# A hybrid decoder step as one list of stages, with compression rows by position and decode parts in column groups

## What is computed

```python
z = rmsnorm(x, pre_norm) @ w_in                 # 3652 columns in layer 0, 6924 in layer 1
# layer 0: differential attention (A, 4 heads, two maps each, softmax1 - lam * softmax2)
#          and indexer-sparse attention (B): the 256 (decode) or 64 (prompt) best keys of
#          score = sum_h w_h * relu(q_idx_h . k_idx), then softmax over those
# layer 1: NSA (C): compressed blocks, selected blocks and a window of 512, mixed by gates,
#          and dilated attention (D): three groups (128, 1), (512, 4), (2048, 16)
def compress(rows, pos_emb, w1, w2):            # C: blocks of 32 rows, 16 apart
    blocks = rows[:, idx] + pos_emb             # (n, 32, 128)
    hid = gelu(einsum('bnrd,rdh->bnh', blocks, w1))
    return hid @ w2
mix = concatenate([o_left * silu(g_left), o_right * silu(g_right)])
y = x + rmsnorm(mix @ w_out, post_norm)
```

## Time and profile before

| | |
|---|---|
| median of 3 runs | 1359.72 us (1356.55 to 1361.18) |
| span of the profiled execution | 1352.9 us; no time of its own beside the span is given for it |
| instructions | 10043 |
| PE busy | 1068.6 us (79%) |
| DVE busy | 417.7 us (31%) |
| ACT busy | 257.1 us (19%) |
| POOL busy | 100.1 us (7%) |
| moved by the transfers | 213.99 MB, a mean of 158 GB/s |

### The profile page before, as it was taken

One profiled execution on the slowest core, in us unless ns is written; L12 is line 12 of the kernel. 1 busy time (PEld: TensorE's weight loads), 2 busy tenths in 40 slices (PEclk: granted clock), 3 DMA queues, 4 the chain that ended last, 5 costly groups with the idle time before them and its releaser, 6 DMA issues.

```text
span 1352.9 us, 10043 instructions
## 1 busy us (share of the span) xinstructions
PE 1068.6 (79%) x3730; PEld 445.2 (33%) x3730; DVE 417.7 (31%) x834; ACT 257.1 (19%) x521; POOL 100.1 (7%) x140
## 2 busy tenths in 40 slices
PE   0799975995995398996675779949999978878586
PEld 0433331221233133332123333323333444455332
DVE  1007655003567021872221310021212144232513
ACT  2511210110025000110030321111010112434112
POOL 2000002001101000001310000010000120100000
PEclk9999986995895589897687879979897965969779
DMA  6424656004999701004836357375444352213330
GB/s 256 162 98 158 241 203 220 0 12 137 360 330 345 275 1 62 1 0 192 367 125 233 131 184 281 123 254 184 171 159 178 101 174 85 86 63 125 94 124 32
DMA packets 71152, 213.99 MB, mean 158 GB/s; under 512 B 6128, under 2 KB 26352, under 8 KB 67648
## 3 DMA queue, kind: packets, MB, share of 16 engines
q0 software_dynamic: 12160, 119.47, 24.0%
q1 hardware_dynamic: 58944, 93.88, 20.4%
HBM read 207.31 MB, written 64.68 MB: 201 GB/s over the span
## 4 chain that ended last, share of the span: by engine, by line
PE 69%; issue 9%; ACT 8%; DVE 6%; DMA 4%; another core or an unknown queue 2%; SPq 1%; ACTq 0%; DVEq 0%
PE psum L580 27%; PE psum L541 14%; PE psum L510 6%; PE psum L764 4%; PE psum L590 3%; PE psum L850 3%; PE psum L672 2%; DMA ring<-in_cmp_w 2%; PE psum L648 2%; PE psum L598 2%; ACT Z L1358 2%; PE psum L521 1%; DMA ring<-in_w_out_even 1%; ACT PT L1232 1%
## 5 line engine op out<-in xcount | busy, mean ns | idle before, releaser
L580 PE MATMUL psum<-ring,XB 128*128 128x512 f32 (+2 forms) x832 | 370.6, 602 | 13.3 <-DMA ring<-in_w_out_even 11.1
L541 PE MATMUL psum<-Z,ring 128*128 128x512 f32 x256 | 225.6, 1038 | 10.9 <-DMA ring<-in_cmp_w 10.9
L580 PEld LDWEIGHTS psum<-ring,XB 128*128 128x128 f32 x832 | 159.2, 199 | 225.1 <-issue 205.4
L1158 ACT COPY Z<-psum 128x512 f32<-128x512 f32 (+3 forms) x78 | 43.6, 559 | 385.1 <-PE psum L580 359.0
L541 PEld LDWEIGHTS psum<-Z,ring 128*128 128x128 f32 x256 | 54.1, 221 | 137.4 <-issue 125.0
L510 PE MATMUL psum<-const,ring 128*128 128x128 f32 (+1 forms) x352 | 71.7, 342 | 9.0 <-issue 4.5
L1501 DVE TENSOR_TENSOR RT<-Z,const 128x256 f32<-128x256 f32 (+10 forms) x25 | 8.7, 347 | 199.2 <-ACT Z L1158 198.5
L510 PEld LDWEIGHTS psum<-const,ring 128*128 128x128 f32 (+1 forms) x352 | 46.8, 165 | 67.2 <-issue 53.2
L1628 DVE CUSTOM_DVE_ANT_0 SM<-psum,const 128x128 f32<-128x128 f32 (+4 forms) x48 | 18.9, 394 | 123.2 <-PE psum L648 118.0
L672 PE MATMUL psum<-Z,PT 128*128 128x128 f32 x168 | 31.6, 335 | 24.5 <-ACT PT L1232 23.6
L590 PE MATMUL psum<-ring,XB 128*32 128x512 f32 (+2 forms) x416 | 50.6, 588 | 0.0
(11 more groups left out here) (286 smaller groups left out, 934.5 us busy)
## 6 DMA issues: line engine op xcount, KB each, us to landing
ring<-in_w_in_odd SPq DMA_DIRECT2D x13, 2048.0 KB, 12.3
ring<-in_cmp_w SPq DMA_DIRECT2D x8, 2048.0 KB, 10.5
ring<-in_w_in_even SPq DMA_DIRECT2D x7, 2048.0 KB, 7.8
out_s_d_k<-in_state_d_k POOLq DMA_DIRECT2D x8, 1022.0 KB, 11.5
out_s_d_v<-in_state_d_v POOLq DMA_DIRECT2D x8, 1022.0 KB, 10.6
ring<-in_w_out_even SPq DMA_DIRECT2D x2, 2048.0 KB, 12.6
ring<-in_state_d_k SPq DMA_DIRECT2D x2, 2048.0 KB, 8.8
ring<-in_state_d_v SPq DMA_DIRECT2D x2, 2048.0 KB, 12.0
```

Of the source, the lines that this page charges most:

```text
L541: last = mm(out[:, h * 512:(h + 1) * 512], w[:, (r % 16) * CH + h * 128:(r % 16) * CH + h * 128 + 128], ap(rowsT[:, r:r + 1], [CS, 512]), ...
L580: last = mm(out[:, 0:n], xT[:, k, t * 128:(t + 1) * 128], w[:, k * n:(k + 1) * n], start=k == 0, stop=k == KT - 1)
L1158: copy(dst, pp[0:dst.shape[0], 0:n]).then_inc(P.free, 1)
```

## The change

- Both layers are one list of stages, `ORDER`, made by `even_order` and `odd_order`. Each engine's program has a function for each kind of stage and goes through that one list. A unit's work is four stages (`prep`, `scores`, `probs`, `output`) that stand in different places of the list.
- Weights have two buffers of 2 MB. Gathered rows and other transfers of about 1 MB have buffers of their own: two fixed ones, and others that are lent for a stretch of the list by tensors that lie idle in it (`homes`).
- `rowsT` becomes 16 planes of 520 columns, one for each position modulo the stride. `compress` reads 512 neighbouring columns; the position vectors stand in column 511 of each plane, and the bias is read from column 511 of the result.
- `decode_rows` gives each of the four groups of output partitions a quarter of the chunk's columns and runs the whole contraction; there is no folding matmul. ACT copies four quarters.
- The keys of shared decode parts go in four column groups, one batch row in each, for 256 keys at a time; softmax then runs on 128 rows.
- Queries reach all partitions by transposes of a repeated column, and for A by a copy to SBUF.
- Chunks are taken in another order, and gates are applied from PSUM before ACT frees the bank (`copy_z`, which is ACT's). The prompt's "sel" units come before "cmp".
- At the start, X, the identity and the rest of the constants are loaded apart, and the page table in one transfer.

```diff
-        items, place, released = [], {}, {}
-
-        def item(name, queue, parts):
-            place[name] = (len(items) % SLOTS, None)
-            items.append((name, queue, parts))
+        def weights(name, parts, at=None):
+            if at is None:
+                at = len([n for n, queue, _ in items if queue == "sp"]) % 2
+            before = [last_weights[at]] if last_weights[at] else []
+            last_weights[at] = name
+            item(name, "sp", parts, f"weights{at}", ring[:, at * 2 * PART:(at + 1) * 2 * PART], before)
...
+        homes = [dict(slot="rows0", view=ring[:, 4 * PART:5 * PART], span=(0, len(ORDER)), before=[], only=None),
+                 dict(slot="rows1", view=ring[:, 5 * PART:6 * PART], span=(0, len(ORDER)), before=[], only=None),
+                 dict(slot="probs", view=PD[:, :], span=(step_of["turn_x", 0, 2], step_of["a_scores", 0]),
+                      before=["turn_x0"], only=None),
+                 dict(slot="heads", view=flat[:, 1024:3072], span=(step_of["scores", 11], step_of["soft", "b"]),
+                      before=["heads_read"], only=None),
...
             def compress(kv):
...
-                        last = mm(out[:, h * 512:(h + 1) * 512],
-                                  w[:, (r % 16) * CH + h * 128:(r % 16) * CH + h * 128 + 128],
-                                  ap(rowsT[:, r:r + 1], [CS, 512]), start=r == 0, stop=r == CB - 1)
+                out, w = turned["out", kv], slot_of(name)
+                at = (r % 16) * PLANE + r // 16
+                for h in range(2):
+                    last = mm(out[:, h * 512:(h + 1) * 512],
+                              w[:, (r % 16) * CH + h * 128:(r % 16) * CH + h * 128 + 128],
+                              rowsT[:, at:at + 512], start=r == BLK_ORDER[0], stop=r == BLK_ORDER[-1])
...
-            def decode_rows(w, n):
-
-                pe.wait_ge(P.free, P.claim())
-                out = P.filling
-                for k in range(KT):
-                    g = 32 * (k % 4)
-                    last = mm(out[g:g + 32, 0:n], xTs[:, k, :], w[:, k * n:(k + 1) * n], start=k < 4, stop=k >= 4)
-                last.then_inc(P.full, 1)
+            def decode_rows_of(w, n):
+
+                pe.wait_ge(T.free, turned["x", 2])
+                pe.wait_ge(P.free, P.claim())
+                out, q = P.filling, n // 4
+                for k in range(KT):
+                    for g in range(4):
+                        last = mm(out[32 * g:32 * g + 8, 0:q], xTs[:, k, :], w[:, k * n + g * q:k * n + (g + 1) * q],
+                                  start=k == 0, stop=k == KT - 1)
+                last.then_inc(P.full, 1)
...
-            def broadcast_query(zs, q, b):
...
-                mm(out[:, :], ap(C("one8", 8)[:, b:b + 1], [0, 128]), zs[0:8, q:q + 512],
-                   start=True, stop=True).then_inc(O.full, 1)
+            def on_all_rows(bank, b):
+
+                pe.wait_ge(T.free, turned["queries"])
+                pe.wait_ge(bank.free, bank.claim())
+                for h in range(H):
+                    last = tr(bank.filling[:, h * 128:(h + 1) * 128], ap(QB[:, h, b:b + 1], [0, 128]))
+                last.then_inc(bank.full, 1)
...
-                        last = mm(out[0:32, half * 512:(half + 1) * 512], QD[0:w, b, :],
-                                  KTs[l][0:w, (i - 1) % 2, :], start=b == 0 and not masked, stop=b == NB - 1)
+                    for q in range(4):
+                        last = mm(DB.filling[32 * q:32 * q + 32, pair * 256:pair * 256 + 256], QD[0:w, 4 * j + q, :],
+                                  KTs[0:w, q, :], start=j + pair == 0 and kind != "c", stop=j + pair == 2)
...
+            def own(kind):
...
+                for b in range(NB):
+                    g = 32 * (b % 4)
+                    last = mm(O.filling[g:g + 32, 0:8], QD[0:w, b, :], KN[0:w, :], start=b < 4, stop=b >= 4)
...
+            def copy_z(l, i, t):
...
+                if w:
+                    act(z[:, c + at:c + at + w], pp[0:n, at:at + w], ACT.Tanh, scale=0.5).then_inc(sem("gate_tanh"), 1)
+                    eng.wait_ge(sem("gate_tanh"), count(sem("gate_tanh")))
+                    eng.wait_ge(sem("gated"), due("act", "gated"))
+                    eng.sem_inc(P.free, 1)
...
+        MOVED_AFTER = dict(ak=1, ck=2, cv=2, dk=2, wk=2, wv=2, ak0_0=0, ak0_1=0, rows1_2=4, bv_3=4)
+        MOVED_AFTER.update({f"ak{b}_{half}": 2 for b in (5, 6, 7) for half in (0, 1)})
...
+                if name == "wout0_1":
+                    sp.wait_ge(*marks["keys_used", "b", TILES["b"] - 1])
+                    load_norm(NW[:, :], "post_norm", 0, "post_in")
+                    sp.wait_ge(*marks["mixed", 0])
+                    load_norm(NWP, "pre_norm", 1, "pre_in")
...
+            for event in ORDER:
+                if event[0] in stages:
+                    stages[event[0]](*event[1:])
```

3169 lines of the change are left out of this document (1662 added, 1507 removed).

## The result

The kernel after takes 935.35 us (median of 4 runs, 930.02 to 937.64), the kernel before 1360.04 us in the same comparison. The ratio is 0.6877, its 95% interval 0.6853 to 0.690.

A forecast was written before the change was run, and what follows sets the result against it. PE work (1068.6 us) and PE idle (284 us) were taken to bound the kernel. Work savings of 194 us gave 875, plus 123 idle made a 998 us span, forecast time 1005 us; range 935 to 1110.

The forecast's parts named there:

- Case A: The forecast itself, whole kernel: PE work 875 plus idle 123 us, total time 950 to 1060 us; chance 0.57.
- case C: Whole kernel, everything covered: idle near 70 us, clock nearly throughout at its upper level, time 900 to 950 us; chance 0.13.
- (1): Compression matmuls: neighbouring reads bring 256 instructions to 0.442 us each, 113 us in all, 112 us gone.
- (2): Position vectors in column 511 of the planes: 128 one-column matmuls go, 12.7 us, with the weight order they forced.
- (3): Shared decode keys in column groups: 61.4 us becomes 17, bounds 14 and 20, so 44 us gone.
- (4): Decode rows of projections in column groups: 77.4 us removed, 62 added (bounds 51 and 74), 15 gone.
- (5): Queries on all rows: 43.4 us of broadcasts replaced by 26 us of transposes and 2 of tiny ones, 15 gone.
- (6): Small additions (own in groups, probabilities turned on 128 rows, 20 transposes): 5 us more.
- (7): PE idle under one stage list and lent buffers: 123 of 284 us stay, 42 in layer 0; bounds 30 and 233.
- Rival B: Lock step: late keys hold DVE, then ACT's gate, then PE; idle stays 21%, 1115 us, range 1060 to 1200; chance 0.20.
- D: Clock falls in light work; query transposes in nearly every gap, 20 more at 3 us, would give 1065; chance 0.05.
- E: Slower: 82 gathered parts on one queue, each landing of 8.7 us exposed, time 1360 us and above; chance 0.04.

The follow-up runs named there:

- strided_in_list: Kernel after, but compression matmuls read 512 columns 16 apart again, same counts and order: 1025.23 us, ratio 0.7591 to before.
- neighbours_in_old: Kernel before, but compression matmuls read 512 neighbouring columns, with order, ring and position vectors unchanged: 1295.25 us, ratio 0.9586 to before.
- query_by_matmul: Kernel after, but a query reaches all partitions by one 8-row broadcasting matmul instead of four transposes: 958.73 us, ratio 0.7083 to before.
- better: Kernel after with only list places changed (index sums, A's own score and norms, decode top-k steps): 906.33 us, ratio 0.6691 to before.
- units_tight: Kernel after, but a prompt unit's four stages stand directly behind one another: 1089.38 us, ratio 0.8054 to before.
- its filled twin: units_tight with four more overwritten matmuls per unit, between its scores and the wait for its probabilities: 1052.46 us.
- after_filled: Kernel after with 47 overwritten matmuls put ahead of 18 of PE's waits: 915.68 us, ratio 0.6763 to before.
- few buffers: Kernel after, but gathered rows have only the two fixed buffers and the spare ones, none lent by other tensors: 999.54 us.
- sums_earlier: better, but the two index-score sums stand ahead of a unit's output instead of behind it: 908.83 us, ratio 0.6725 to before.

## Why the prediction came out as it did

**What bounds the kernel** was read rightly: PE's work and PE's idle time. Case A's waits came (129.6 us for 123), and with them part of case C's clock (0.93 for 0.85 before); C wanted both idle near 70 and the clock up. The time itself, 935 us, lies below A's own 950 to 1060 and in C's 900 to 950. That it falls into the stated range by less than 1 us is luck. Of the prediction's own signs, the compression line (0.469 us), idle time under 140 us and no long wait on compression weights came; PE's busy time, 798.6 us and not 855 to 895, didn't, and the decode rows lie just below their 51 to 74.

**(1) Compression by position**, right: forecast -112, measured 225.6 - 120.1 = 105.5, and shown from both sides by strided_in_list and neighbours_in_old.

**(2) Position vectors**, right: the line (12.7 us) and the order that it forced are gone.

**(3) Keys**, right: 18.3 us for a forecast of 17.

**(4) Decode rows**, mis-sized: 62 us forecast, 49.6 measured, below even the bound of 51. The bounds were a row with 512 columns cut to a quarter and a row of the decode values; the row that was nearest, 16 instructions in 0.45 us, 28 ns each, was used only to say that issue doesn't bind. It was the price: 30 ns. The Trainium skill's 62 ns a matmul for software decode (TensorE: Matmul & The Clock Gate, section "Wait — 56ns, not 53.3ns?") isn't borne out by this trace.

**(5) Queries**, right in sign and mis-sized: the transposes cost 19.7 us and not 26. What wasn't priced at all is that the 8-row broadcasts slowed what stood around them; query_by_matmul puts this at 20 us of busy time besides the line's own 20.

**(6)** is small and wasn't tested apart.

**(7) Idle time**, right in sum. Start, passage, layer 1 and end were each within about 5 us. Layer 0 kept 60.8 us and not 42: VectorE is busy for 265 of 437 us there, and for 78 of the 100 us from 160 to 260. The version better took 14.5 us of idle time away there (46.3 us are left). Rival B saw the place rightly and overrated it.

**The step that failed** is the sum of (1) to (6) "1068.6 becomes 875". It prices each removed and added instruction and leaves all others at what they cost before. The parts (1) to (5) gave 213 us (105.5, 12.7, 43.1, 27.8 and 23.7) where the sum had 199, and that is 14 of the missing 76. The other 62 stand in lines for which the sum had no term but 5 us of additions: they fell by 57 us, and 47 of these are their part of the slow sum, 71.4 before and 24.0 after. So most of what was missing is the clock, in light work that the change leaves as it was. The projections gained nothing from it (370.6 and 370.8). The last 15 us, the 10 that these lines lost beside the clock and the 5 that (6) was to cost, no run explains.

That waits lower the clock and so make later work dear is shown by units_tight, its filled twin and after_filled, and by the nearly constant rest of five kernels. How the 47 us split between the removed waits and the removed broadcasts isn't settled: query_by_matmul puts back only the broadcasts, in the new order, for 24 us of slow sum, 6 of them in the broadcasts themselves; the 52 folding matmuls of the old order (L598) were put back by no run.

**The rivals.** B: the late keys that hold DVE, ACT's gate and then PE weren't seen at its scale; units_tight, whose waits have another cause, came out near its 1115, at 1089 us. C was the nearest in time: with its idle time of 70 us the sum gives 875 + 70 + 7 = 952, so its 900 to 950 leaves the clock up to some 50 us, and 47 came; its chance was 0.13. D is refuted for transposes and holds for broadcasts, of which the change removes most. E: transfers of gathered values are exposed for 3.7 us at most in the kernel after, and for up to 8.0 with few buffers.

## What to carry to other kernels

Price idle time twice. Where the granted clock is below 1 in the old profile, add busy time x (1 - clock) over short slices, leave out work that doesn't move with the clock, and count the share of it that stands behind removed waits as a gain of its own; a change that closes waits makes untouched work behind them cheaper. Count it line by line: here the light groups gained 47 us and the projections, by far the largest line, none. If a wait can't be closed, dummy matmuls in it pay only while long waits stand ahead of work that is sensitive to the clock: here 37 us on a kernel full of them, some 15 us on the kernel after, nothing on sums_earlier. Read a moving operand's spacing from the duration per column before anything else, and move such a part together with the order that feeds it.

## What the runs showed of the hardware

- An fp32 matmul that reads 512 columns 16 elements apart takes 0.88 to 0.95 us an instruction, at either level of the clock; with neighbours it takes 0.44 us at the upper level.
- Small matmuls of 128 x 8 by 128 into four column groups run at 30 ns each, 1664 of them in 49.6 us.
- Sixteen broadcasts from 8 rows, 9.69 us without a wait, are followed by projections at 10.13 us a block; 96 dense transposes or matmuls of 128 x 128 by 128, 10.6 and 10.9 us, are followed by 7.03. So the granted clock fell in stretches in which PE was never idle, and what stood in them made the difference.
- The granted clock fell from 1.00 to 0.50 at the end of a wait of 2.4 us (at 433.5 us of the kernel after) and was back at 447 us; whether the thin broadcasts behind the wait kept it down isn't shown.
